# A seven that waits for its parts one by one, and seven more sevens in place of plain products

## The reference

```python
def swiglu(xn, w_gate, w_up, w_down):
    return (jax.nn.silu(xn @ w_gate) * (xn @ w_up)) @ w_down

x = x + swiglu(rms_norm(x, ffn_norm[layer]), w_gate[layer], w_up[layer], w_down[layer])
```

## Time and profile before

| | |
|---|---|
| three runs, median | 2063.2 us (2061.11, 2063.20, 2063.71) |
| the profiled execution | 2061.32 us, its span 2059.5 us |
| PE busy | 2049.4 us, 100%, 9087 matmuls |
| DVE busy | 1709.5 us, 83% |
| ACT busy | 1125.5 us, 55% |
| DMA | 452.72 MB, mean 220 GB/s; mean busy share 6 to 8 tenths in most slices |
| granted TensorE clock | 1.000 over the whole span |

### The profile page before, as it was taken

How to read it: one execution, slowest core, us unless ns; L and a number is a source line. 1 busy time by engine, 2 the same in 40 slices (tenths; PEclk the granted TensorE clock), 3 DMA queues, 4 the chain that set the end, 5 groups by cost and what they waited for, 6 DMA issues and landing times.

```text
span 2059.5 us, 26502 instructions
## 1 busy us (share of the span) xinstructions
PE 2049.4 (100%) x9087; PEld 1694.9 (82%) x9087; DVE 1709.5 (83%) x2251; ACT 1125.5 (55%) x1417; POOL 76.6 (4%) x85
## 2 busy tenths in 40 slices
PE   9999999999999999999999999999999999999999
PEld 7888888888888888888888888888888888888887
DVE  5777669799999998878876777597999999988887
ACT  6465555555555555545555566555555555545453
POOL 0100011000000000000011000010000000000000
PEclk9999999999999999999999999999999999999999
DMA  8788766767776777766677775567677776776664
GB/s 276 218 278 254 210 205 205 217 204 226 225 240 215 234 224 234 220 210 204 197 233 242 234 229 154 196 200 217 214 213 236 215 244 213 235 234 205 223 200 160
DMA packets 252307, 452.72 MB, mean 220 GB/s; under 512 B 17840, under 2 KB 51760, under 8 KB 252208
## 3 DMA queue, kind: packets, MB, share of 16 engines
q1 hardware_dynamic: 249760, 447.24, 70.4%
q10 hardware_dynamic: 2448, 4.21, 0.6%
HBM read 422.81 MB, written 28.57 MB: 219 GB/s over the span
## 4 chain that ended last, share of the span: by engine, by line
PE 96%; DVE 2%; DMA 1%; issue 1%; ACT 0%; SPq 0%; DVEq 0%; ACTq 0%
PE psum L972 21%; PE psum L974 21%; PE psum L973 21%; PE psum L844 9%; PE psum L847 9%; PE psum L845 9%; PE psum L912 1%; PE psum L898 1%; DMA w_raw<-in_w_down 1%; PE psum L864 0%; DMA w_raw<-in_ab_w_in 0%; DMA w_raw<-in_w_up 0%; DVE w_lo L1472 0%; ACT w_hi L1079 0%; DVE xt_lo L1930 0%
## 5 line engine op out<-in xcount | busy, mean ns | idle before, releaser
L1079 ACT ACTIVATE w_hi<-w_raw 128x1024 fp32r<-128x1024 f32 x665 | 696.3, 1057 | 584.5 <-PE psum L974 244.4
L1472 DVE TENSOR_TENSOR w_lo<-w_raw,w_hi 128x1024 fp32r<-128x1024 f32 x587 | 707.6, 1221 | 223.2 <-ACT w_hi L1079 222.0
L974 PE MATMUL psum<-w_hi,xt_lo 128*128 128x512 f32 x1060 | 412.7, 389 | 0.0
L972 PE MATMUL psum<-w_hi,xt_hi 128*128 128x512 f32 x1060 | 412.7, 389 | 0.0
L973 PE MATMUL psum<-w_lo,xt_hi 128*128 128x512 f32 x1060 | 412.7, 389 | 0.0
L844 PE MATMUL psum<-w_hi,xt_hi 128*128 128x512 f32 x604 | 243.2, 403 | 0.8 <-DVE w_lo L1472 0.8
L847 PE MATMUL psum<-w_hi,xt_lo 128*128 128x512 f32 x604 | 235.9, 391 | 0.0
L1152 ACT ACTIVATE ht_hi<-stages 128x1024 fp32r<-128x1024 f32 x116 | 123.2, 1062 | 205.5 <-DVE stages L1911 185.1
L845 PE MATMUL psum<-w_lo,xt_hi 128*128 128x512 f32 x604 | 235.5, 390 | 0.0
L973 PEld LDWEIGHTS psum<-w_lo,xt_hi 128*128 128x128 f32 x1060 | 199.1, 188 | 41.4
L974 PEld LDWEIGHTS psum<-w_hi,xt_lo 128*128 128x128 f32 x1060 | 199.1, 188 | 41.1
(11 more groups left out here) (249 smaller groups left out, 2678.6 us busy)
## 6 DMA issues: line engine op xcount, KB each, us to landing
w_raw<-in_w_gate SPq DMA_DIRECT2D x176, 512.0 KB, 4.6
w_raw<-in_w_up SPq DMA_DIRECT2D x176, 512.0 KB, 4.1
w_raw<-in_w_down SPq DMA_DIRECT2D x176, 512.0 KB, 5.3
w_raw<-in_cd_w_in SPq DMA_DIRECT2D x80, 512.0 KB, 4.6
w_raw<-in_ab_w_in SPq DMA_DIRECT2D x71, 512.0 KB, 4.5
block_dram<-turn_sb SPq DMA_DIRECT2D x42, 512.0 KB, 5.1
w_raw<-in_ab_w_out SPq DMA_DIRECT2D x32, 512.0 KB, 4.6
w_raw<-in_cd_w_out SPq DMA_DIRECT2D x32, 512.0 KB, 4.1
```

The costliest lines, as they stand in the source:

```text
L972: nc.tensor.matmul(acc, a_hi, b_hi, start=start, stop=False)
L974: return nc.tensor.matmul(acc, a_lo, b_hi, start=False, stop=stop)
L1079: nc.scalar.activation(w_hi[:, slot, 0:n, :], w_raw[:, slot, 0:n, :], ACT.Copy).then_inc(hi_ready, 1)
L1472: nc.vector.tensor_tensor(w_lo[:, slot], w_raw[:, slot], w_hi[:, slot].bitcast(F32), ALU.subtract).then_inc(lo_ready, 1)
```

## The change

Four things change.

1. `SEVEN`: the first layer's twins get 6 and 5 sevens (before 5 and 4), the second layer's 6 and 8 (before 5 and 6). `UP_FIRST_SEVEN`: the first up and gate tile that uses sevens, once a layer, gets three (before two).
2. `seven_products` waits in more steps and in another order: its first two block products wait for `seven_split`, a new semaphore that `split_seven` increments; then come two products that use only the first half of the weight sums; then the one on unit b; then the last two.
3. `sum_lows` makes one half a call; the second half's call now stands behind `split_lower`.
4. `BLOCKS_AT`, `OUT_AT`, `BACK_AT` and `PARTS_AT` move to other units.

```diff
-SEVEN = (((6, 9, 12, 15, 18), (5, 8, 11, 14)), ((6, 9, 12, 15, 18), (3, 6, 9, 12, 15, 18)))
+SEVEN = (((6, 8, 11, 13, 16, 18), (4, 7, 9, 12, 14)), ((5, 8, 10, 13, 15, 18), (2, 4, 6, 9, 11, 14, 16, 18)))
...
-BLOCKS_AT, OUT_AT, BACK_AT, PARTS_AT = (TU - 1, TU + 16), (TU + 6, TU + 24), (TU + 12, TU + 30), (TU + 15, TU + 33, 2 * TU - 1)
+BLOCKS_AT, OUT_AT, BACK_AT, PARTS_AT = (TU - 1, TU + 19), (TU + 10, TU + 26), (TU + 16, TU + 30), (TU + 18, TU + 34, 2 * TU - 1)
...
-UP_FIRST_SEVEN = UP_SEVEN[1:]
-UP_ROWS = UP_FIRST_SEVEN + UP_SEVEN[:1]
+UP_FIRST_SEVEN = UP_SEVEN
+UP_ROWS = UP_SEVEN
...
-                    pe.wait_ge(lo_ready, u + 1)
+                    pe.wait_ge(seven_split, s + 1)
                     own(only_bank(odd, 0), rows, p, 0, 0, w_hi[:, a, 0, :], w_lo[:, a, 0, :], first, last)
                     mm = own(bank_of(odd, 0, 0), rows, p, 1, 0, w_hi[:, a, 1, :], w_lo[:, a, 1, :], False)
                     mm.then_inc(unit_used, 1)
+                    pe.wait_ge(s_ready, rows_done)
+                    pe.wait_ge(tl_ready, s * 2 + 3)
+                    sums_product(0, 0, 1)
+                    sums_product(2, 1, 3)
                     pe.wait_ge(lo_ready, u + 2)
-                    pe.wait_ge(s_ready, rows_done)
                     mm = three(bank_of(odd, 1, 0), s_hi_of[:, 3, :], s_lo_of[:, 3, :], w_hi[:, b, 1, :], w_lo[:, b, 1, :],
                                False)
                     mm.then_inc(unit_used, 1)
                     pe.wait_ge(tl_ready, s * 2 + 4)
...
                         if seven and j == 0:
                             other_sums(u, i % RING, down_sum(layer, d, p), sums,
                                        lambda: row_lows(down_rows(layer, d, p), rows_raw, rows_of[0][:], rows_of[1][:]))
-                            sum_lows(down_sum(layer, d, p), sums)
+                            sum_lows(down_sum(layer, d, p), sums, 0)
                         if seven and j == 1:
                             split_lower(u, i % RING)
+                            sum_lows(down_sum(layer, d, p), sums, 1)
```

More of the change, by code:

```diff
@@ L419, in encoder @@
         t2_summed = sem("t2_summed")
+        seven_split = sem("seven_split")
         rows_step = sem("rows_step")
@@ L985, in seven_products, with sums_product @@
                     s_hi_of, s_lo_of = lows
-                    pe.wait_ge(lo_ready, u + 1)
+                    def sums_product(k, t, which):
+                        three(only_bank(odd, which), s_hi_of[:, k, :], s_lo_of[:, k, :], t_hi_of[:, t, :], t_lo_of[:, t, :],
+                              first, last)
+                    pe.wait_ge(seven_split, s + 1)
                     own(only_bank(odd, 0), rows, p, 0, 0, w_hi[:, a, 0, :], w_lo[:, a, 0, :], first, last)
@@ L995, in seven_products @@
                     pe.wait_ge(tl_ready, s * 2 + 4)
-                    for k, t, which in ((0, 0, 1), (2, 1, 3), (1, 2, 2)):
-                        three(only_bank(odd, which), s_hi_of[:, k, :], s_lo_of[:, k, :], t_hi_of[:, t, :], t_lo_of[:, t, :],
-                              first, last)
+                    sums_product(1, 2, 2)
                     own(bank_of(odd, 0, 1), rows, p, 1, 1, t_hi_of[:, 3, :], t_lo_of[:, 3, :],
@@ L1466, in split_seven @@
                 dve.wait_ge(hi_ready, u + 1)
-                nc.vector.tensor_tensor(w_lo[:, slot], w_raw[:, slot], w_hi[:, slot].bitcast(F32), ALU.subtract)
+                nc.vector.tensor_tensor(w_lo[:, slot], w_raw[:, slot], w_hi[:, slot].bitcast(F32),
+                                        ALU.subtract).then_inc(seven_split, 1)
             def split(u, slot):
@@ L1922, in other_sums, with sum_lows @@
                 nc.vector.tensor_tensor(raw[:, 3, :], w_raw[:, a, 1, :], raw[:, 2, :], ALU.subtract).then_inc(lo_ready, 1)
-            def sum_lows(s, sums):
+            def sum_lows(s, sums, half):
                 raw, high, low = sums
[L1927 to L1931, removed]
+                dve.wait_ge(th_ready, s * 2 + (half + 1))
+                two = slice(2 * half, 2 * half + 2)
+                nc.vector.tensor_tensor(low[:, two, :], raw[:, two, :], high[:, two, :].bitcast(F32),
+                                        ALU.subtract).then_inc(tl_ready, 1)
             def split_lower(u, b):
@@ L1953, in up_tile @@
                     if twin and p in up_sevens(i) and j == 1:
-                        sum_lows(up_sum(layer, i, UP_SEVEN.index(p)), UP_T)
+                        sum_lows(up_sum(layer, i, UP_SEVEN.index(p)), UP_T, 0)
                         split_lower(u, idx % RING)
+                        sum_lows(up_sum(layer, i, UP_SEVEN.index(p)), UP_T, 1)
                     elif twin and p in up_sevens(i):
```

## The result

| | before | after |
|---|---|---|
| median of 16 runs each | 2063.35 us (2060.84 to 2065.80) | 2066.62 us (2064.27 to 2068.86) |
| ratio | | 1.0018, 95% interval 1.0011 to 1.0024 |
| the profiled execution, its span | 2061.32, 2059.5 us | 2065.40, 2063.6 us |

The forecast was 2063.0 and no change. The time lies in the range given, but the direction was missed: the interval excludes no change. The profiled executions differ by 4.1 us.

A forecast was written before the change was run, and what follows sets the result against it. PE, busy for 2049.4 of 2059.5 us, was taken as the bound: number of matmuls times their distance, plus waits. The terms -4.8 - 3.7 + 2.7 + 4.9 + 0.6 gave -0.3 us, 2063 for a median; range 2056.5 to 2067.5.

The forecast's parts named there:

- Matmuls removed: On PE, the added sevens save 21 matmuls at 0.2267 us each, 4.8 us in all.
- Old stalls: PE waits of before, 1.0 us in the up stage and 2.7 in the first layer's second twin, 3.7 counted.
- The 2-gap's period: Sevens two double chunks apart ask 11.4 us of DVE where PE needs 10.2; under 10.8 or over 12 means wrong.
- What a seven asks of its lead: In the down twins, DVE's first sums must start 4.3 us before a seven's first matmul; 5.8 before the change.
- The 3-gap gives back 0.6: Sevens three double chunks apart return 0.6 us of lead to DVE, with bounds of 0.2 to 1.8.
- The last twin's first 2-gap: Second layer's second twin, sevens 2 to 4: period taken as 11.4 us, leaving seven 4 a margin of 0.9.
- the slower rival: Down twins: the load's landing binds 2-gaps once over 4.9 us; at 6.15 the kernel takes 2075 us; chance 0.10.
- The prediction's own bad end for this twin: Last twin: 5.5 us of stalls with 2-gaps of 11.8 and 3-gaps giving back 0.2.
- First layer, second twin: Its new stalls sum to 4.9 us, at sevens 9, 12 and 14; ends at 0.9 and 9.
- The two first twins: Each layer's first down twin gets 0.3 us of new stalls, 0 to 1 each, 0.6 in the sum.
- The finer waits: PE's waits in a seven: later waits give each seven 1.5 us more margin; bounds for this gain 0 to 2.0.
- they give nothing: Rival on the finer waits: the second half comes as late as it is needed; +6.7, 2069.7 us; chance 0.03.

The follow-up runs named there:

- light_loads: Kernel after, weight loads of the second layer's second twin fetching only 256 of 512 columns; 2060.26 us, ratio 0.9993 to the kernel before.
- moved_norm: Kernel after with one BLOCKS_AT and one PARTS_AT entry moved, so the norm's work lies outside seven 9 of the first layer's second twin; 2062.46 us, ratio 0.9997.
- last_twin_old: Kernel after with the six sevens of before, not eight, in the second layer's second twin; 2060.61 us, ratio 0.9991 to the kernel before.
- fine_only: Kernel before with only the finer waits and the new order of the sums' lo, sevens and norm's places unchanged; 2059.41 us, ratio 0.9985.
- more_only: Kernel before with only the new sevens and the new places of the norm's work, old waits and DVE order; 2071.75 us, ratio 1.0047.
- one_wait: Kernel after with PE's last two waits of a seven moved up to the wait for the first half; 2076.69 us, ratio 1.0074 to before.

## Why the forecast was off

The forecast had 8.2 us of new stalls; 13.4 came. The steps that failed are two landing times in the last twin: that of the load that ends a 3-gap, and that of the load that ends the first 2-gap. Step by step:

- **Matmuls removed, 4.8**: right (9087 to 9066; distance 0.2267 in the down stages wherever nothing waits).
- **Old stalls, 3.7**: right in place; 4.2 measured.
- **The 2-gap's period, 11.4**: right, 11.30, in four of the last twin's five; the first and one of the first layer (12.72, from seven 12 to seven 14) are over the 12 that was named as a sign of being wrong. The Trainium skill's rule that the next Vector instruction starts only when the pipe is empty (VectorE: DVE Perf Modes, "The DRAIN you can't avoid") would have made it 12.6 by recorded durations; the same section allows an earlier start to an instruction that isn't held, and that is what the rows show: from L1937 to L1886 1.13 for a record of 1.22. The half microsecond of idleness ahead of `split_lower` is 0.57.
- **What a seven asks of its lead, 4.3**: near. In the table below sevens with 3.8 us lose 0.7 to 1.1, one with 4.7 loses 0.2.
- **The 3-gap gives back 0.6: this step failed.** The two of the last twin gave 15.88 and 15.44, on the mean 15.66: nothing. `split_lower` and the splits behind it did move by what the prediction said: the load is issued 10.0 us behind the first sums (9.4 before, by the earlier trace rows). The burst was looser, too, and the load landed in 5.8 and 5.4 us instead of 6.0 to 6.5. But 15.04 needs 5.0; what the landing gained, the later issue took. The row of before said 15.62 with 1.09 of idleness, and `light_loads` shows that the loads alone hold back 2 us of each 3-gap.
- **The last twin's first 2-gap: this step failed as well.** It was taken at 11.4 and took 13.28. Its load needed 6.6 us, where it decides once it takes over 4.9; that was the slower rival, given a tenth. It came true in this 2-gap and the first layer's of 12.72, but not in the other four of the last twin (4.3 to 4.4 us). That it is a matter of loading is shown (`light_loads`: 11.29 there); the stores in flight with it are the likely reason, not tested.
- **The sum of the last twin closes**: forecast from first sums 2 to first sums 18, 5 x 11.4 + 2 x 15.04 = 87.1; measured 1944.51 to 2034.31 = 89.8, 2.7 more: 1.9 from the first 2-gap, 1.2 from the 3-gaps, less 0.4 from the other 2-gaps. Stalls of this twin 5.6 for 2.7, 2.9 more. The prediction's own bad end for this twin was 5.5.

The last twin of after by sevens; the lead is the time from a seven's first sums on DVE to its first matmul, the stall what PE's distances add to 0.2267 us within it and to the first matmuls behind it:

| seven | 2 | 4 | 6 | 9 | 11 | 14 | 16 | 18 |
|---|---|---|---|---|---|---|---|---|
| lead measured, us | 6.4 | 3.3 | 3.8 | 4.2 | 3.8 | 4.7 | 3.8 | 3.8 |
| stall forecast | 0 | 0 | 0.3 | 0 | 0.6 | 0 | 0.6 | 1.2 |
| stall measured | 0 | 1.5 | 0.7 | 0.6 | 0.7 | 0.2 | 1.1 | 0.7 |

- **First layer, second twin, 4.9**: 6.2. Forecast at 9, 12 and 14: 1.9, 1.4, 1.6; measured 3.0, 1.1, 2.1. The place and the cause of the longest wait were right (`moved_norm`), and so was what that seven asks: lead 4.1 and stall 3.0 make 7.1, for the 7.0 forecast. Too large was the lead at the twin's start: 7.25 at seven 4 for 8.2, because its first sums waited 0.85 us for a load with a block transfer behind it. In `last_twin_old`, whose first layer is the same, seven 4 has 8.2, seven 9 stalls 2.0, and the twin loses 4.2. So the 1.3 us of miss here is within what single profiles vary. The bound of 7.65 for a landing was counted from the block transfer's issue at 966.26; the load itself was released at 965.8 and took 8.1 to the first sums.
- **The two first twins, 0.6**: 1.3.
- **The finer waits**: worth 3.1 us alone and some 6 with the new sevens (7.0 argued). That they give nothing is refuted by `fine_only`, `more_only` and `one_wait`.
- **The sum's own sign**: -0.3 forecast, +4.4 by stages. The last twin is 2.9 of the miss, the first layer's second 1.3, the two first twins 0.7. That the time still lies in the range owes something to its width: the stalls came out 5 us over the forecast's.

## What to carry to other kernels

- Where an item needs a lead and spends some of it, write down per interval which resource sets its period: here DVE over the short gap, the landing over the long one. Here the row that showed an idle wait for data in the long gap also said that this gap gives nothing back, at a busy share of 80%.
- Before adding more of the cheap items, free the ones that are there: moving two groups of small transfers away from a seven's loads was worth 1.3 to 3.3 us, while the seven further sevens took 4.8 us of matmuls away and, with the old waits, made the kernel 9.7 us slower.
- If a consumer's waits are made finer, look at the order in which the helper engine makes the parts as well: ACT's swap was worth some 8 us here with the new sevens, and nothing where no seven was late.

## What the runs showed of the hardware

- A stop of PE costs more than the lateness of what it waits for. At 1963.24 and 1965.54 the part was there 0.62 and 0.09 us after PE could have gone on, and 0.85 and 0.26 were lost: the matmul starts 0.15 or 0.05 us behind the end of the part's instruction, its record is 0.47 or 0.50 us for 0.39, and the next one starts 0.31 or 0.34 behind it for 0.23. So each stop adds some 0.2 us. In the last twin after, the waits shown are 0.8 us and the loss is 5.6.
- A load of 512 KB lands in 4.3 to 4.4 us where its neighbours are issued 2.4 us or more away from it (four 2-gaps of the last twin after), in 5.4 to 5.8 where they are 1.1 us before and 1.7 behind it (its 3-gaps; 6.0 to 6.5 in before's), and in 6.6 with two stores in flight.
- Single executions of one kernel differ by stage by 1 to 2 us (down 1, with the same code, 237.20 to 239.02; down 2 of `moved_norm` and of after 236.76 and 235.64), so a stage of one profile tells effects of over 2 us.
